# A page of cached keys or values on 64 partitions, two neighbouring keys on each, in place of one key on each of 128

## What is computed

```python
k_past = cache_k[page_table].reshape(DB, -1, H, Dh)          # 8 pages of 128 keys a sequence
v_past = cache_v[page_table].reshape(DB, -1, H, Dh)
R = (lax.cumsum(lf_past, axis=1, reverse=True) - lf_past).transpose(0, 2, 1)
s_past = jnp.einsum('bqhd,bkhd->bhqk', q, k_past) * scale + Fn[..., None] + R[:, :, None, :]
p = jax.nn.softmax(jnp.concatenate([s_past, s_new], axis=-1), axis=-1)
out = jnp.einsum('bhqk,bkhd->bqhd', p[..., :P], v_past) + ...
```

## Time and profile before

| What | Value |
|---|---|
| Median of 3 runs | 1989.72 us (1985.43 to 1995.66) |
| The profiled execution, its own time | 1988.57 us |
| Its span, first to last instruction | 1987.0 us, 28,107 instructions |
| Busy: PE, PE weight load, DVE, ACT, POOL | 90%, 56%, 27%, 11%, 8% |
| DMA | 530.85 MB, mean 267 GB/s, 150,457 packets |
| Cached pages | 64 DMAs of keys, 64 of values, 512 KB each, 5.9 and 5.7 us from issue to landing |
| Mean granted clock of TensorE | 0.952 of full speed |

### The profile page before, as it was taken

How to read it: one execution, slowest core, us unless ns; L and a number is a source line. 1 busy time by engine, 2 the same in 40 slices (tenths; PEclk the granted TensorE clock), 3 DMA queues, 4 the chain that set the end, 5 groups by cost and what they waited for, 6 DMA issues and landing times.

```text
span 1987.0 us, 28107 instructions
## 1 busy us (share of the span) xinstructions
PE 1791.8 (90%) x11118; PEld 1121.3 (56%) x11118; DVE 532.0 (27%) x1145; ACT 209.1 (11%) x403; POOL 158.5 (8%) x274
## 2 busy tenths in 40 slices
PE   6589999999998999996888999998699998989898
PEld 3145666666666786764667777775333333333334
DVE  2020000000008654445555111002423322332223
ACT  2010000000001110111222100002210001000102
POOL 1011021111101000240000000000100000000000
PEclk9789999999999999997899999999799899989999
DMA  9997776685814433627999884323399999999991
GB/s 356 421 354 284 254 266 242 232 318 177 289 43 143 141 97 122 215 87 282 392 392 359 330 300 133 127 94 160 101 376 414 391 405 384 403 391 398 387 379 48
DMA packets 150457, 530.85 MB, mean 267 GB/s; under 512 B 17701, under 2 KB 61899, under 8 KB 123611
## 3 DMA queue, kind: packets, MB, share of 16 engines
q1 hardware_dynamic: 124980, 432.32, 57.3%
q0 software_dynamic: 17088, 97.15, 13.9%
q10 hardware_dynamic: 8336, 0.66, 0.3%
HBM read 510.94 MB, written 19.15 MB: 267 GB/s over the span
## 4 chain that ended last, share of the span: by engine, by line
PE 73%; DMA 14%; DVE 5%; SPq 3%; issue 3%; DVEq 1%; ACT 1%; POOLq 0%; POOL 0%; ACTq 0%
PE ps L627 70%; DMA ring<-in_w_up_e_dram 4%; DMA xT<-in_w_ada_dram 4%; DMA ring<-in_w_ada_dram 3%; PE ps L637 2%; DMA xT<-in_w_in_dram 2%; SPq L384 2%; SPq L378 1%; DVE z L1383 1%; DVE ring L1380 1%; DVE z L1374 1%; DMA z<-in_x_sample_dram 0%; DVEq L2006 0%; DVE ring L1470 0%; DVE ring L1374 0%
## 5 line engine op out<-in xcount | busy, mean ns | idle before, releaser
L627 PE MATMUL ps<-hT,ring 128*128 128x288 f32 x2304 | 585.6, 411 | 9.5 <-ACT hT L1196 6.0
L627 PEld LDWEIGHTS ps<-hT,ring 128*128 128x128 f32 x2304 | 432.8, 191 | 167.8 <-issue 55.2
L627 PE MATMUL ps<-ring,work 128*64 128x512 f32 (+1 forms) x1280 | 279.4, 638 | 36.6 <-DMA ring<-in_w_ada_dram 24.8
L627 PE MATMUL ps<-z,ring 128*128 128x288 f32 (+1 forms) x1040 | 257.5, 408 | 4.5 <-PE ps L627 2.7
L1383 DVE COPY z<-ps 128x256 f32<-128x256 f32 (+7 forms) x98 | 64.4, 660 | 692.5 <-PE ps L627 671.8
L627 PE MATMUL ps<-ring,z 32*32 32x256 f32 (+3 forms) x3744 | 219.3, 402 | 21.3 <-DVE z L1383 11.2
L627 PEld LDWEIGHTS ps<-z,ring 128*128 128x128 f32 x1040 | 197.7, 191 | 62.4 <-issue 6.1
L627 PEld LDWEIGHTS ps<-ring,work 128*64 128x64 f32 (+1 forms) x1280 | 77.9, 135 | 203.8 <-issue 164.3
L627 PEld LDWEIGHTS ps<-ring,z 32*32 32x32 f32 (+3 forms) x3744 | 109.5, 115 | 119.7 <-issue 112.7
L1196 ACT ACTIVATE z<-ps 128x512 f32<-128x512 f32 (+4 forms) x108 | 60.1, 602 | 919.5 <-PE ps L627 909.8
L1380 DVE SCALAR_TENSOR_TENSOR xT<-ps,modT,xT 128x256 f32<-128x256 f32 x160 | 70.8, 480 | 260.1 <-PE ps L627 260.1
(11 more groups left out here) (201 smaller groups left out, 822.8 us busy)
## 6 DMA issues: line engine op xcount, KB each, us to landing
ring<-in_w_in_dram SPq DMA_DIRECT2D x36, 2048.0 KB, 12.9
xT<-in_w_ada_dram POOLq DMA_DIRECT2D x64, 1024.0 KB, 7.3
ring<-in_w_gate_e_dram SPq DMA_DIRECT2D x32, 2048.0 KB, 12.8
ring<-in_w_up_e_dram SPq DMA_DIRECT2D x32, 2048.0 KB, 18.3
ring<-in_w_down_e_dram SPq DMA_DIRECT2D x32, 2048.0 KB, 14.4
ring<-in_w_ada_dram SPq DMA_DIRECT2D x16, 2048.0 KB, 26.1
ring<-in_cache_k_dram SPq DMA_DIRECT2D x64, 512.0 KB, 5.9
ring<-in_cache_v_dram SPq DMA_DIRECT2D x64, 512.0 KB, 5.7
```

Source lines behind the costliest of these rows:

```text
L627: return nc.tensor.matmul(o, lhsT, rhs, start=start, stop=stop, skip_group_check=free)
```

## The change

Each page goes to one half of the partitions: pages 0 and 2 of a slot to partitions 0 to 63, pages 1 and 3 to partitions 64 to 127. Two neighbouring keys (8 KB, contiguous in the page) lie on one partition, and a pair of pages shares 2048 columns of the slot. All else that reads the slots is unchanged. The permutation of the forget sums is changed to the new places, in eight DVE copies of 128x256, read with a stride of two floats, in place of two copies of 128x1024. ACT's output pattern is left alone, so the probabilities come out in the order in which the values now lie.

```diff
--- before.py
+++ after.py
@@ -381,8 +381,9 @@
 
                             sp.wait_ge(*step("gla_scratch_free"))
                         sp.wait_ge(sem(f"ring_free{s}"), b + freed_for_pages(s))
-                    sp.dma_start(slot(s)[:, n * 1024:(n + 1) * 1024],
-                                 io[name][0, ds(pg, 1)].rearrange("a p h d -> (a p) (h d)")).then_inc(sem(f"kv_full{s}"), 16)
+                    pair, upper = n // 2, n % 2
+                    sp.dma_start(slot(s)[64 * upper:64 * upper + 64, pair * 2048:(pair + 1) * 2048],
+                                 io[name][0, ds(pg, 1)].rearrange("a (p r) h d -> (a p) (r h d)", r=2)).then_inc(sem(f"kv_full{s}"), 16)
 
 
             def late_gate_weights(b):
@@ -1780,7 +1781,11 @@
             turn_keys(0, 1, 4, False)
             for g in range(2):
                 v.wait_ge(sem(f"r_rep_full{g}"), 64)
-                copy(r_turn[:, g, :].rearrange("p (a n i) -> p a n i", a=4, n=NPG), r_rep[:, g, :].rearrange("p (n a i) -> p a n i", n=NPG, a=4))
+                key_of = r_turn[:, g, :].rearrange("p (u a q r i) -> p u r a q i", u=2, a=2, q=NPG // 2, r=2)
+                page_of = r_rep[:, g, :].rearrange("p (q u a i r) -> p u r a q i", q=NPG // 2, u=2, a=2, r=2)
+                for u in range(2):
+                    for r in range(2):
+                        copy(key_of[:, u, r], page_of[:, u, r])
             v.drain()
             v.sem_inc(sem("r_turn_ready"), 1)
             find_max(0)
```

## The result

| | Before | After |
|---|---|---|
| Median | 1988.84 us (4 runs, 1985.43 to 1995.66) | 2110.55 us (4 runs, 2092.97 to 2118.68) |
| Ratio, 95% interval | | 1.060 (1.0562 to 1.0638) |
| Profiled execution, its span | 1988.57, 1987.0 us | 2092.97, 2091.3 us |
| DMA packets | 150,457 | 142,265 |
| Sequence: late weights to late weights | 24.4 us | 39.9 us |

The profile after is of the fastest of the four runs (the others took 12 to 26 us more), so its terms sum to less than the medians' difference. Its table by stretches has the columns of the earlier trace rows: busy time and count of PE, PEld, DVE, ACT, POOL, then granted clock, DMA share and GB/s.

A forecast was written before the change was run, and what follows sets the result against it. The prediction took the cache-page stage to be bound by its transfers, TensorE about 3 us a sequence behind. Pages 112, keys 4, copies 1.1 and what follows 2 made +119 us on 1988.6: 2108 us, range 2040 to 2135.

The forecast's parts named there:

- What bounds: Stage of cache pages: bound by its transfers at 24.4 us a sequence, TensorE about 3 us a sequence behind.
- 64 partitions, 2.28 us a page: Transfer-bound stretch: a page on one half takes 2.28 us, not 1.28; 112 page DMAs add 112 us.
- The gather: First gather of routed rows, alone on 64 partitions: 230 GB/s per full share of busy, used to price a page.
- Keys of sequence 0: Start of the stage: slot 0's pages stay hidden, slot 1's four pages on the chain add 4.0 us.
- The copies: Table of forget sums before r_turn_ready: eight DVE copies take 2.4 us where two took 1.30, adding 1.1 us once.
- The last values: End of the stage: eight last value pages take longer but stay just hidden behind TensorE's work.
- The +2 for what comes behind: After the last value pages: gates read back and second up weights come later, charged 2 us (0 to 8).
- The sum: Whole kernel: 112 + 4 + 1.1 + 2 = +119 us on 1988.6, making 2108 us, 6% slower.
- Other signs: Changed profile: 8,192 packets fewer, sequences of 40 us, about 240 GB/s, TensorE waiting about 19 us, pages landing in 10 to 12.
- SP stays ahead: SP's queue in the stage: a page is issued in about 1.2 us, so SP's issuing does not bound.
- B: Rival for the stage: the halves partly overlap, a page takes 1.76 us, total 2046 us; chance 0.28.
- C: Rival for the stage: halves served side by side at full rate, page at most 1.28 us, 1985 us; chance 0.12.

The follow-up runs named there:

- e11: Kernel before with only the value pages sent to halves of the partitions, keys unchanged: 2052.78 us, ratio 1.032 to the kernel before.
- e2: Changed kernel with each page on every second partition instead of one half, rows of 8 KB: 2001.99 us, ratio 1.005 to the kernel before.
- e8: e2 without the look-up of page numbers, reading fixed pages: 1984.90 us, ratio 0.998 to the kernel before.
- e5: Changed kernel with a slot's pages issued two for the lower half, then two for the upper, not alternating: 2122.82 us, ratio 1.067 to the kernel before.
- e6: e3 with its pages issued so that lower and upper half alternate: 2112.36 us, ratio 1.064 to the kernel before.
- e1: Changed kernel with two rows of 4 KB a partition in place of one of 8 KB: 2113.03 us, ratio 1.061 to the kernel before.
- e3: Changed kernel with each page on one quarter of the partitions, 32 with rows of 16 KB: 2127.97 us, ratio 1.068 to the kernel before.
- e10: Kernel before with the late gate weights issued by ACT in place of SP: 2010.38 us, ratio 1.010 to the kernel before.

## Why the prediction was right

*What bounds.* The forecast has the stage bound by its transfers and the page slower on one half. Shown: the DMA share stays at 1.03 to 1.04 in every stretch, the loss is a sum over pages (e11), and it goes away when the 64 partitions are spread (e2, e8).

*64 partitions, 2.28 us a page.* From r_turn ready (908.5 before, 917.4 after, from the DVE rows) to the last late weights (1084.9 and 1194.6) went 176.4 and 277.2 us: +100.8, or 0.90 for each of 112 pages, where 1.00 was forecast; in the steady part it is (39.9 - 24.4)/16 = 0.97. The gather read 230 GB/s for each full share; the stage gave 223 (230/1.03) in its first stretch and 245 (255/1.04) in the last shown. That a stream of alternating halves would behave as a lone gather was a guess. In order, the stage gave 218 (227/1.04, e5), alternating a few per cent more, so that the gather's figure was near by some luck.

*Keys of sequence 0.* From SP's first issue to landing 8.8 us before (891.27 to 900.08) and 12.4 after (896.16 to 908.6): +3.6, forecast +4.0.

*The copies.* Eight in 1.72 us, two had taken 1.30: +0.4, forecast +1.1. The row taken for the price (256 elements on 32 partitions, 0.30 each) was too dear; these cost 0.21.

*The last values.* From the last late weights to their use 34.6 us before (1084.9 to 1119.52) and 34.6 after (1194.62 to 1229.26), and the next up tiles start 6.0 us later in both: hidden, as forecast. The +2 for what comes behind was not needed.

*The sum.* 3.6 + 0.4 + 100.8 = 104.8. The unchanged code ahead of the stage ran 4.9 us longer in this execution (SP's issue at 896.2, not 891.3) and that behind it 5.4 shorter (from the first up tile after the values to the end: 861.5 and 856.0). That gives the 104.3 by which the two spans differ. The forecast was +119: against this profile the 112 pages were put 11 us too high and the +2 was not needed. The median of the runs moved by 122, since the profiled run was the fastest and the others took 12 to 26 us more. No profile shows where they spent it, so that the median came out within 3 us of the forecast is in part luck.

*Other signs.* 8,192 packets fewer, exactly. 40 us a sequence, 240 GB/s: met. TensorE's wait was put at 19 us a sequence, it is 17 (119.1 over 7). Landing of pages was put at 10 to 12 us; values have 11.4, keys 15.9. SP's DMA instruction grew from 0.33 to 0.48 us, which the prediction did not see ("SP stays ahead" held because the transfers were so slow; e2 shows SP as the bound once they are not).

*Rivals.* B (1.76 us a page) and C (1.28 or less) both fall: the stage never passed 255 GB/s. An effect in B's direction is likely (e5, e6), at most a quarter of what B needs: from the 42.4 us of e5 to the 39.9 of the changed kernel, where 16 pages of 1.76 us and the other 3.9 would make 32.1. C's time (1985 us) is that of e8 (1984.90), but there each DMA reaches both halves by itself; side by side, as C had it, two DMAs didn't get there.

## What to carry to other kernels

In these runs a DMA's rate hung on which partitions it touched: 64 spread ones were as fast as 128, and 64 neighbours about as slow as 32, with rows of 4 to 16 KB. So spread a narrow tile over all partitions by a step (`slot[u::2]`) rather than laying it in one half. Look at GB/s beside the DMA share, since a share of 1 says only that the engines are occupied. The nearest lone transfer in the old trace was a good price for the change. When the shape of a DMA changes, recount the issuing engine's time too. And before a load of short rows goes to a second queue beside long ones, ask what waits for it.

## What the runs showed of the hardware beside that

SP's time for one DMA instruction of 512 KB differed with its shape: 0.33 us for 128 rows of 4 KB, 0.48 for 64 rows of 8 KB, 0.60 for 64 partitions with two rows of 4 KB, 0.32 for 32 rows of 16 KB. From the views of line 385 of e1 and line 384 of e3 (shortest, median and longest in ns):

```profile
L385 SPq DMA_DIRECT2D ring<-in_cache_k_dram x64: 598/602/873, 866.8 to 1167.0; - x64
```

```profile
L384 SPq DMA_DIRECT2D ring<-in_cache_k_dram x64: 315/316/1217, 864.7 to 1172.6; - x64
```

Two queues did not share the engines by bytes: 1 MB in rows of 512 B took 27 us to land beside 8.66 MB in rows of 4 KB in another queue (e10, its queue lines above), and 9.4 us in its place in the same queue.
